# A two-block transformer forward pass: one tile of the second mixer's input projection is multiplied ahead of the norm's roots

## The reference

```python
x = first_block(x, ...)                       # ends: return rms_norm(h, final_norm)
mod = (c_act @ w_ada[l] + b_ada[l])[:, None, :]
shift1, scale1, gate1, shift2, scale2, gate2 = jnp.split(mod, N_MOD, axis=-1)
h = _rmsnorm(x, g_mix[l]) * (1.0 + scale1) + shift1
proj = h @ w_in[l]
a_u, a_v, b_q, b_k, b_v, c_q, c_k, c_v = jnp.split(proj, splits, axis=-1)
...
x = x + (1.0 + gate1) * y
h = _rmsnorm(x, g_ffn[l]) * (1.0 + scale2) + shift2
up = _causal_dwconv(h @ w_up[l], conv_w[l], conv_b[l])
```

## Time and profile before

| | |
|---|---|
| median of three runs | 1739.95 us |
| the profiled execution | 1740.24 us |
| its span | 1738.5 us |
| mean granted clock of TensorE | 0.997 of full |
| TensorE matmul busy | 1716.6 us (99%), 7866 instructions |
| VectorE busy | 1140.0 us (66%) |
| ScalarE busy | 702.2 us (40%) |
| GpSimd busy | 398.4 us (23%) |
| chain that ended last | TensorE 89%, VectorE 6%, ScalarE 2%, issue 2% |

### The profile page before, as it was taken

One profiled execution on the slowest core, in us unless ns is written; L12 is line 12 of the kernel. 1 busy time (PEld: TensorE's weight loads), 2 busy tenths in 40 slices (PEclk: granted clock), 3 DMA queues, 4 the chain that ended last, 5 costly groups with the idle time before them and its releaser, 6 DMA issues.

```text
span 1738.5 us, 22097 instructions
## 1 busy us (share of the span) xinstructions
PE 1716.6 (99%) x7866; PEld 1398.8 (80%) x7866; DVE 1140.0 (66%) x1440; ACT 702.2 (40%) x960; POOL 398.4 (23%) x170
## 2 busy tenths in 40 slices
PE   9999999999999999999999999999999999999998
PEld 6888888888887888878888888888757888888886
DVE  7566777777556797677777666653766777777222
ACT  5123444444233556444444432432464544444221
POOL 4444100000554340210000054454302300000441
PEclk9999999999999999999999999999999999999999
DMA  5233222322754230132222265422201232322231
GB/s 212 97 109 97 97 97 97 97 97 73 266 212 151 91 98 7 53 105 96 97 97 97 83 256 218 149 97 86 85 1 46 76 109 97 97 97 97 97 109 49
DMA packets 52188, 186.34 MB, mean 107 GB/s; under 512 B 5920, under 2 KB 6048, under 8 KB 52128
## 3 DMA queue, kind: packets, MB, share of 16 engines
q1 hardware_dynamic: 51552, 184.34, 31.0%
q10 hardware_dynamic: 576, 1.20, 0.2%
HBM read 183.41 MB, written 2.10 MB: 107 GB/s over the span
## 4 chain that ended last, share of the span: by engine, by line
PE 89%; DVE 6%; ACT 2%; issue 2%; DMA 1%; DVEq 0%; SPq 0%; ACTq 0%
PE ps L1630 27%; PE ps L1631 27%; PE ps L1632 27%; PE ps L1836 1%; PE ps L1837 1%; PE ps L1838 1%; DVE RAB L1190 1%; DVE acc L986 1%; PE ps L1958 1%; PE ps L1947 0%; PE ps L1694 0%; DVE XL L997 0%; PE ps L2069 0%; DMA X<-x_in 0%; PE ps L1689 0%
## 5 line engine op out<-in xcount | busy, mean ns | idle before, releaser
L532 POOL TENSOR_TENSOR WL<-raw,WH 128x1024 fp32r<-128x1024 f32 x157 | 387.2, 2468 | 1297.3 <-ACT WH L577 1297.3
L1630 PE MATMUL ps<-XH,WH 128*128 128x512 f32 x1472 | 575.9, 391 | 0.2 <-DVE XL L1548 0.2
L1631 PE MATMUL ps<-XL,WH 128*128 128x512 f32 x1472 | 572.8, 389 | 0.0
L1632 PE MATMUL ps<-XH,WL 128*128 128x512 f32 x1472 | 572.8, 389 | 0.0
L577 ACT ACTIVATE WH<-raw 128x1024 fp32r<-128x1024 f32 x291 | 307.9, 1058 | 506.4 <-PE ps L1632 461.9
L1630 PEld LDWEIGHTS ps<-XH,WH 128*128 128x128 f32 x1472 | 276.3, 188 | 60.7 <-issue 2.1
L1632 PEld LDWEIGHTS ps<-XH,WL 128*128 128x128 f32 x1472 | 276.3, 188 | 57.7
L1631 PEld LDWEIGHTS ps<-XL,WH 128*128 128x128 f32 x1472 | 276.4, 188 | 57.4 <-issue 1.0
L1630 PE MATMUL ps<-HH,WH 128*128 128x512 f32 x528 | 205.4, 389 | 0.0
L1631 PE MATMUL ps<-HL,WH 128*128 128x512 f32 x528 | 205.4, 389 | 0.0
L1632 PE MATMUL ps<-HH,WL 128*128 128x512 f32 x528 | 205.4, 389 | 0.0
(11 more groups left out here) (310 smaller groups left out, 2030.0 us busy)
## 6 DMA issues: line engine op xcount, KB each, us to landing
raw<-w_tiles SPq DMA_DIRECT2D x291, 512.0 KB, 3.3
ada<-ada_tiles SPq DMA_DIRECT2D x32, 512.0 KB, 4.4
trig<-ada_tiles SPq DMA_DIRECT2D x16, 512.0 KB, 5.7
X<-x_in SPq DMA_DIRECT2D x4, 512.0 KB, 6.8
out_x<-X SPq DMA_DIRECT2D x8, 256.0 KB, 2.0
RAB<-c_in SPq DMA_DIRECT2D x2, 512.0 KB, 4.5
MK<-mask_in ACTq DMA_DIRECT2D x1, 640.0 KB, 3.8
trig<-rope_in SPq DMA_DIRECT2D x2, 256.0 KB, 2.9
```

Of the source, the lines that this page charges most:

```text
L532: nc.gpsimd.tensor_tensor(WL[k % SPL][:, :], raw[:, k, :], f32(WH[k % SPL][:, :]), ALU.subtract).then_inc(s_lo, 1)
L1630: mm(bank, h, xh, start=first, stop=False)
L1631: mm(bank, h, xl, start=False, stop=False)
L1632: return mm(bank, lo, xh, start=False, stop=last)
```

## The change

The columns of the projection are laid out anew: `IN2R`'s first tile becomes `IN2A`, a phase of its own ahead of the groups. It is multiplied by the scaled X (without the root) in the order of UP2, the sums stand behind its chunk 3, the spreads behind its chunks 5 and 7. XH and XL hold the scaled inputs, and `modulated` overwrites them chunk by chunk once TensorE has signalled `s_gone`. The last chunk's squares are now added on VectorE like the others, and the fillers are gone. IN2A is tile 24 of the count above, IN2 has 25 to 32. ScalarE's scaled copies stand around the rounding of tile 26, chunks 0 to 2 before it and 3 to 6 behind it, and the rounding of tile 27 stands behind the roots. VectorE's seven subtractions for them stand behind `vectors`, ahead of the last `X[:, m]`. Semaphores and the renumbering that follows from the new phase are left out below, as is the evict of UP2, which calls the same helper `moved_result`.

```diff
@@ -86,7 +86,7 @@
     ("UP1", 2 * FF, [1]), ("DN1", 24, [0, 0, 1]),
-    ("IN2", 8, [0, 0, 0, 4]), ("IN2R", 2, [1]), ("IN2F", 12, [1]), ("OUT2", 8, [1]), ("UP2", 2 * FF, [1]), ("DN2", 24, [0, 0, 1]),
+    ("IN2A", 1, [1]), ("IN2", 8, [0, 0, 0, 4]), ("IN2R", 1, [1]), ("IN2F", 12, [1]), ("OUT2", 8, [1]), ("UP2", 2 * FF, [1]), ("DN2", 24, [0, 0, 1]),
@@ -616,7 +624,14 @@
                         for j in range(tiles_per_m - late):
+                            if second and late and j == 1:
+                                act.wait_ge(s_gm, 1)
+                                for u in range(3):
+                                    scaled_hi(u)
                             ahead(T0[phase] + k * tiles_per_m + j, i, per)
+                        if second and late:
+                            for u in range(3, KD - 1):
+                                scaled_hi(u)
@@ -632,7 +647,9 @@
                                 .then_inc(s_sq2, 1)
-                        if late:
+                            if m == KD - 1:
+                                scaled_hi(m)
+                        if late and not second:
@@ -851,15 +868,18 @@
             nc.scalar.activation(nt[:, 2:4, :], nt[:, 0:2, :], ACT.Sqrt, scale=1.0 / D).then_inc(s_root, 1)
+            ahead(T0["DN1"] + 3 * KD - 1)
...
-            def modulated(nb0, shift):
+            def modulated(nb0, shift, gone=None):
...
                     act.wait_ge(s_nb, nb0 + m + 1)
+                    if gone is not None:
+                        act.wait_ge(*((s_gone, m + 1) if m < KD - 1 else (s_pe, gone)))
@@ -867,7 +887,7 @@
                         nc.scalar.activation(XH[:, m, :], MB[m % 4], ACT.Copy).then_inc(s_xh, 1)
-            modulated(NB_M2, 0)
+            modulated(NB_M2, 0, DONE_T[T0["IN2A"]])
@@ -1008,15 +1028,22 @@
+            def scaled_lo(m):
...
+                lo_half(XH[:, m, :], XL[:, m, :], X[:, m, :], gm[:, 0, m:m + 1], (s_gxh, GX_FIN + m + 1), s_gxl)
...
+            def moved_result(dst, bank, i):
...
+                dve.wait_ge(s_moved, i + 1)
+                v.reduce_sum(epsc[:, 1 + i:2 + i], ps[6][:, 0:2], AX_X).then_inc(s_first, 1)
+                v.tensor_tensor(dst, bank, rb[:, :], ALU.mult).then_inc(s_first, 1)
+                dve.wait_ge(s_first, 2 * (i + 1))
+                return v.tensor_scalar(dst, dst, epsc[:, 1 + i:2 + i], None, ALU.add)
...
-                at_end = APART.index(n)
-                dve.wait_ge(s_early, 2 + at_end)
-                if n == N_FIN:
-                    ch.link(v.tensor_scalar(nt[:, 6, :], ps[5][:, 0:4], D * EPS, None, ALU.add))
-                    ch.link(v.scalar_tensor_tensor(nt[:, 7, :], nt[:, 6, :], EPS, ps[5][:, 4:8], ALU.mult, ALU.add))
-                else:
-                    ch.link(v.tensor_copy(nt[:, 6, :], ps[5][:, 0:4]))
+                dve.wait_ge(s_early, 1)
+                ch.link(v.tensor_copy(nt[:, 6, :], ps[5][:, 0:4]))
@@ -1034,6 +1061,8 @@
                             last()
+                            for u in range(KD - 1):
+                                scaled_lo(u)
@@ -1050,11 +1079,13 @@
                         if n == N_F2:
-                            lo_half(QXH[:, m, :], QXL[:, m, :], X[:, m, :], gm[:, 1, m:m + 1], (s_gxh, m + 1), s_gxl)
+                            lo_half(QXH[:, m, :], QXL[:, m, :], X[:, m, :], gm[:, 1, m:m + 1], (s_gxh, GX_F2 + m + 1), s_gxl)
...
                             v.tensor_tensor(rbl[:, :], rbl[:, :], AT[:, k % 2, :], ALU.add).then_inc(s_acc2, 1)
+                            if m == KD - 1:
+                                scaled_lo(m)
@@ -1372,15 +1399,18 @@
                     ch.link(v.tensor_scalar(gm[:, row, :], mod[:, part * KD:(part + 1) * KD], 1.0, None, ALU.add))
-                ch.link(v.tensor_tensor(gm[:, 0, :], gm[:, 0, :], vec[:, V["final"][0]:V["final"][0] + KD], ALU.mult))
+                v.tensor_tensor(gm[:, 0, :], gm[:, 0, :], vec[:, V["final"][0]:V["final"][0] + KD], ALU.mult).then_inc(s_gm, 1)
+                dve.wait_ge(s_gm, 1)
+                for half in range(2):
+                    b = mod[:, 3 * half * KD:(3 * half + 1) * KD]
+                    ch.link(v.tensor_copy(shift[:, half, :, 0], b))
+                    v.tensor_tensor(shift[:, half, :, 1], b, f32(shift[:, half, :, 0]), ALU.subtract).then_inc(s_shift, 1)
...
             dve.wait_ge(s_ssum, N_FIN + 2)
-            ch.step(v.tensor_tensor(nt[:, 0, :], nt[:, 6, :], ps[4][:, 0:4], ALU.add))
-            ch.step(v.tensor_tensor(nt[:, 1, :], nt[:, 7, :], ps[4][:, 4:8], ALU.add))
-            ch.wait()
-            v.scalar_tensor_tensor(nt[:, 1, :], ps[4][:, 0:4], EPS, nt[:, 1, :], ALU.mult, ALU.add).then_inc(s_ms, 1)
+            ch.link(v.tensor_scalar(nt[:, 0, :], ps[4][:, 0:4], D * EPS, None, ALU.add))
+            v.scalar_tensor_tensor(nt[:, 1, :], nt[:, 0, :], EPS, ps[4][:, 4:8], ALU.mult, ALU.add).then_inc(s_ms, 1)
@@ -1403,8 +1433,9 @@
             modulated(E_M2, NB_M2, 0, 0, ps[4])
-            ch.link(v.tensor_copy(shift[:, :, 0], mod[:, 3 * KD:4 * KD]))
-            v.tensor_tensor(shift[:, :, 1], mod[:, 3 * KD:4 * KD], f32(shift[:, :, 0]), ALU.subtract).then_inc(s_shift, 1)
+            ch.link(v.tensor_copy(rb[:, :], ps[4][:, :]))
+            product(M0["IN2A"])
+            moved_result(AT[:, 0, :], ps[5][:, :], 0).then_inc(s_ev, 1)
@@ -1442,8 +1473,10 @@
                         v.tensor_copy(dst[:, n, :], ps[(first + n) % 4][:, :]).then_inc(s_ev, 1)
-                elif k in (8, 9):
-                    to_aux(k - 8, M0["IN2R"] + k - 8)
+                elif k == 8:
+                    pass
+                elif k == 9:
+                    to_aux(1, AUX_M[1])
@@ -1658,24 +1691,23 @@
-            def ahead_of_root(t, M, n):
...
-                bank_free(M)
-                pe.wait_ge(s_shift, 1)
+            def ahead_of_root(t, bank, half, src, gx, sums, spreads):
...
+                tile_ready(t)
+                pe.wait_ge(s_shift, half + 1)
...
                     for w in (WH, WL):
-                        move = mm(ps[6][:, 0:2], w[t % SPL][:, k * P:(k + 1) * P], shift[:, k, :],
+                        move = mm(ps[6][:, 0:2], w[t % SPL][:, k * P:(k + 1) * P], shift[:, half, k, :],
...
                         move.then_inc(s_moved, 1)
-                    pe.wait_ge(s_gxl, k + 1)
-                    last = dot(ps[M % 4][:, :], t, k, QXH[:, k, :], QXL[:, k, :], k == 0, k == KD - 1)
-                    if k == 2:
-                        pe.wait_ge(s_acc, ACC0[n + 1])
-                        token_squares(acc, 0)
-                    if k == 3:
-                        spread(3, ps[4], 4)
-                last.then_inc(s_pe, 1)
+                    pe.wait_ge(s_gxl, gx + k + 1)
+                    last = dot(bank, t, k, src[0][:, k, :], src[1][:, k, :], k == 0, k == KD - 1)
+                    last.then_inc(*((s_gone, 1) if k < KD - 1 else (s_pe, 1)))
+                    if k in sums:
+                        sums[k]()
+                    if k in spreads:
+                        spread(*spreads[k])
@@ -1971,19 +2008,14 @@
-            pe.wait_ge(s_acc, ACC0[N_FIN + 1])
-            token_squares(acc, 0, ps[5], s_early)
-            pe.wait_ge(s_acc2, KD + 1)
-            token_squares(rbl, 4, ps[5], s_early)
-            pe.wait_ge(s_sq, SQ0[N_FIN + 1])
-            token_squares(SQ[:, 1, :], 0)
-            pe.wait_ge(s_sq2, KD)
-            token_squares(AT[:, 1, :], 4)
-            awake(6)
-            spread(2, ps[4], 5)
-            spread(2, ps[7], 4)
-            awake(4)
             n_in = 22
...
+            def both_sums():
...
+                pe.wait_ge(s_acc, ACC0[N_FIN + 1])
+                token_squares(acc, 0)
+                pe.wait_ge(s_acc2, KD + 2)
+                token_squares(rbl, 4)
@@ -2082,14 +2114,17 @@
             for k in range(n_in):
-                if k in (0, 4):
-                    token_group(T0["IN2"] + k, M0["IN2"] + k, 4, S, block_of, inputs(E_M2) if k == 0 else None)
-                elif k in (8, 9):
-                    wide(T0["IN2R"] + k - 8, M0["IN2R"] + k - 8)
+                if k == 0:
+                    ahead_of_root(T0["IN2A"], ps[5][:, :], 0, (XH, XL), GX_FIN, {3: both_sums},
+                                  {5: (2, ps[4], 5), 7: (2, ps[7], 4)})
+                elif k in (1, 5):
+                    token_group(T0["IN2"] + k - 1, M0["IN2"] + k - 1, 4, S, block_of, inputs(E_M2) if k == 1 else None)
+                elif k == 9:
+                    wide(T0["IN2R"], M0["IN2R"])
...
                 if k in (9, 10):
-                    turn(k - 9, M0["IN2R"] + k - 9)
+                    turn(k - 9, AUX_M[k - 9])
```

More of the change, by code:

```diff
@@ L137, in build @@
         epsc = sb("epsc", [P, 16])
-        shift = sb("shift", [P, KD, 2], F32R)
+        shift = sb("shift", [P, 2, KD, 2], F32R)
         gsgu = sb("gsgu", [P, A_W])
@@ L331, in build @@
         s_first = sem("s_first")
+        s_gm = sem("s_gm")
+        s_gone = sem("s_gone")
         s_knh = sem("s_knh")
```

(45 more changed lines are left out.)

## The result

The changed kernel is slower: 1742.79 us, the median of 20 runs, against 1740.15 us for the old one in as many; the ratio is 1.0014 (95% interval 1.0008 to 1.002), so 2.4 us, with 1.4 to 3.5 in the interval (the two medians differ by 2.6). The forecast was 1739.9 with a range up to 1742.4. The profiled execution took 1742.18 us with a span of 1740.5. The effect is 0.14% of the time, so a single execution has to be read with care: at DN1's last product this one already stands 1.5 us behind the old one, in a part of the kernel that the change does not touch.

The account below looks back on a forecast made before the run. PE was taken as busy throughout, with 10.94 us without a product between DN1 and IN2. Order -2.5, clock +2.9 and turn -0.4 sum to 0.0 against the profiled 1740.24 us, so 1739.9 us at the median, range 1735.0 to 1742.4.

Parts of the forecast that it names:

- The term that decides: GpSimd and VectorE before IN2: GpSimd holds lo(3), seven subtractions precede X[7], which ends 4.2 us late; PE waits 3.0 us.
- clause on the clock: Between DN1 and IN2 the clock falls at about 1116.5, slowing squares and products: 2.1 to 3.8 us, 2.9 taken.
- the sum: Whole kernel: -2.5 + 2.9 - 0.4 = 0.0 us against the profiled execution, 1740.24 us.
- -2.5: At IN2's start, before the clock's cost: IN2 starts at 1124.4 against 1126.91, a gain of 2.5 us.
- The turn: Behind IN2, first turns' wait for AT: 0.1 to 0.3 us instead of 0.4, and no late start; counted as -0.4 us.
- the mark to beat is 1121.47 + 5.44 = 1126.91: IN2's old first product plus one tile of 5.44 us: when the old order had done as much work.
- 0.3 above the median of the runs shown: Step from the profiled execution, 1740.24 us, to the median of the runs, giving the forecast 1739.9 us.
- mark for "no change": Whole kernel: 0.2%, 3.5 us, is about what a measurement can tell from no change.
- Rival 1: Before IN2 the sums are late but the clock holds: -2.9 us, 1737.0 us; chance 13%.
- Rival 2: GpSimd doesn't hold VectorE at lo(3), IN2 starts at 1122.6: -4.7 us, 1735.2 us; chance 15%.
- Rival 3: Clock stays low into IN2, rising at 1130: 3.4 us more, 1743.3 us, slower; chance 7%.

Follow-up runs that it names:

- round_later: Changed kernel with the rounding of tile 26 moved behind the roots: ratio 0.9992 to the old kernel, median 1740.24 us.
- sums_first: Changed kernel with the last X, its squares and both sums ahead of scaled chunks 3 to 6: ratio 0.9989 to the old kernel, again 0.9982.
- fillers: Changed kernel with 18 filler matmuls in PE's wait for acc: ratio 0.9999 to the old kernel, median 1740.67 us.
- old_warm: Old kernel with ten more fillers between its four sets of squares: ratio 1.0 to the old kernel, edge 9.69 us.
- old_1: Old kernel unedited, timed against itself and profiled again: ratio 0.9999, edge 8.96 us.

## Why the prediction was wrong

**Right, within a few tenths (on the changed kernel, with its 1.5 us of lateness taken off).** Chunks 0 to 2 subtracted in GpSimd's idle time; lo(3) stands behind GpSimd; X[7] at 1115.0 (forecast 1115.0); acc begins at 1116.4 and is whole at 1117.1 (1117.1); lo(3) lasts 2.37 us (2.3); PE waits 2.8 us (3.0); rbl whole at 1117.7; IN2's first product at 1127.6 (1127.3). The term that decides was the right one, and round_later and sums_first show it: GpSimd's hold (4.36 us where 2.7 are needed, so 1.7) and the wait for XH between the two groups of subtractions (0.7) are 2.4 us of X[7]'s lateness, and with the sums first the whole edge is 6 us shorter. Without its clause on the clock the sum was exact at the edge: -2.5 forecast, -2.5 with the fillers.

**The clock.** It fell at 1119.4 and rose at 1126.2, so at 1117.9 and 1124.7 on the old scale; the forecast had the fall at 1116.5 and the rise between 1121.5 and 1124.9. A chunk took 1.8 us at 1.2 GHz, a product 0.43 from start to start (1122.41 to 1122.84) against 0.227 at full clock (5.44 over 24), so 1.9, as taken. The price was 3.2 us by fillers, against the 2.9 of the sum and inside its 2.1 to 3.8. The middle was a little low because the clock fell 1.4 us later than forecast, when the squares were under way, so that all 6.8 us of it had work of PE in them (an estimate: 6.8 times 0.48 is 3.3).

**The turn.** -0.2 measured, or -0.25 by all profiles, -0.4 forecast. The reason held: VectorE's L1465, the old L1434, took 0.43 us, and the copy came 0.2 us late:

```profile
1179.93 0.43 DVE L1465 TENSOR_SCALAR RAB<-RAB 128x512 f32<-128x512 f32 x1
...
1183.79 0.68 DVE L1210 COPY AT<-ps 128x512 f32<-128x512 f32 x1
```

**The step that failed is "the mark to beat is 1121.47 + 5.44 = 1126.91".** It took the old edge, 10.94 us, from one execution in which the clock was low for 6.8 us of it. In four further executions it is 9.34 on average. The mark held 2.5 to 2.8 us of low clock (10.94 against the 8.1 to 8.4 estimated at full clock), where the old order loses 1.3 to 1.6 on average. The clause on the clock charged the new order what it does lose in every run and left the old order's own loss as one execution had it. At full clock on both sides, by that estimate, the new order gains nothing at the edge: 8.42 against 8.1 to 8.4. The -2.5 of the sum was the mark's low clock; what the order of the lists cost, sums_first shows (8.42 against 5.60).

The sum against the profiled execution was nearly right (0.0 forecast, +0.5 found at the edge and the turn), and the sum against the median, which is what was asked, lacked 1.3 us for the mean of the old edge. These 1.8 us are what is shown of the 2.4 measured; some 0.6 stay open, as said above. The step from the profiled execution to the median ("0.3 above the median of the runs shown") didn't help: in that execution a cheap first half, 2 us ahead of most others at 1017 us, stood against the dear edge. And 3.5 us was too coarse a mark for "no change": twenty runs of each kernel told 2.4 us from zero.

**The rivals.** Rival 1 (the clock holds) did not occur in four profiles; fillers produced it: its edge was as priced, its time, ratio 0.9999, was 2.7 us above what the rival had, of which the dear mark explains 1.3. Rival 2 (GpSimd does not hold VectorE) is false, and round_later shows what it would have given, but for a low clock of 3.4 us: the edge 3.9 us sooner, where the rival had 4.7. The trace of the kernel before could have settled it. There 32 subtractions of this form, with X and XH in SBUF, stand on one line: the eight that met GpSimd idle took 0.75 us, the 24 that began beside it took 1.51 to 2.38, and each of these ended 0.55 us behind GpSimd's subtraction (count, then shortest, median and longest in ns):

```profile
L997 DVE SCALAR_TENSOR_TENSOR XL<-X,vec,XH x32: 748/2112/2383, 7.7 to 751.5; 128x512 fp32r<-128x512 f32 x16, - x16
```

Rival 3 (slower, by a clock that stays low into IN2) gave the sign but not the place: in all four profiles the rise came before IN2's first product.

## What to carry to other kernels

A stage in which PE has no products has a price that depends on the clock, and a single profile shows one draw of it: before an edge is taken as the mark to beat, read it in several executions, or price it once with the clock at 1.00 and once at 0.50, on both sides of the comparison. When work is moved into a wait, the instructions that feed the end of the wait go first in every engine's list, and the new work behind them; here the same tile made the edge 2 us dearer in one order and 4 us cheaper in the other (2.4 slower and 1.9 to 3.1 faster by the times). Look also at what runs beside the engine that has become the path: a subtraction on GpSimd that was free in its old place held VectorE for 1.7 us in the new one.

## What the runs showed of the hardware

The clock also falls in places that the change does not touch, in some executions only: for 3.4 to 6.8 us within the first 17 us (fillers, round_later, sums_first, old_warm), and for 3.4 to 6.8 us from about 554 us on (in 8 of the 14 profiles). PE has waited there for `acc`, 1.6 to 3.4 us in all 14; in the old profile's chain `acc` is late behind a rounding of ScalarE, and that behind the landing of its weight tile (4.47 us from its issue). ScalarE's rounding there begins between 548.0 and 550.6 us, according to when the tile lands. Together these put the engines 0.2 us ahead of the first old profile to 4.6 us behind it at 1017 us, for old and changed kernels alike, and nothing is added from there to DN1's end. In the last 3 to 6 us of every span the clock is at 0.50 too, which changes nothing in the time: the stretch behind the edge is the same within 0.1 us.

The fall follows the last product by different times: 2.3 us in the first old profile, 5.1 in old_1 (1116.2 against 1111.1), 3.7 in the changed kernel (1119.4 against 1115.7, where the next product would have started before the wait). In round_later a wait of 0.4 us with squares behind it was followed by 3.4 us of low clock; in sums_first the same squares without a wait left it at 1.00 in both of its profiles. In the old kernel squares and small matmuls did not keep it up: it fell in all five profiles, with PE busy for the whole time from DN1's end to the fall in four of them and for 5.03 of 5.10 us in old_1.
